# First attention: rotary score products of heads 4 to 7, two heads at a time on the two halves of the rows

## The chip, the cores and the metric

One core of one Trainium2 chip runs the whole program. Times are device microseconds (us) of one execution. In the rows PE is TensorE (matmuls), PEld its weight loads, DVE VectorE, ACT ScalarE, POOL GpSimd, SP the queue that issues most loads.

## What is computed

Two transformer blocks one after the other in fp32, cut here to the part that matters: the attention of the first block's second layer (512 tokens and 256 context tokens, so 768 keys). It has eight heads. Heads 0 to 3 have a head dimension of 128 and share two key/value heads. Heads 4 to 7 have a part without rotary embedding (128 wide, keys of its own for each head) and a rotary part (64 wide, one key for all four heads).

```python
Q_BLOCK = 128; C_HEADS = 4; C_HEAD_DIM = 128; D_HEADS = 4; D_NOPE = 128; D_ROPE = 64; D_V = 128

def block_attention(q, k, v, scale):          # for each block of 128 queries and each head
    sc = einsum('bqhgd,bkhd->bhgqk', qblk, k).astype(float32) * scale
    p = softmax(sc, axis=-1)
    return einsum('bhgqk,bkhe->bqhge', p, v)

def cd_attend(q, qdn, qdr, k, v, kdn, kdr, vd):
    oc = block_attention(q.reshape(b, L, C_KV_HEADS, C_GROUP, C_HEAD_DIM), k, v, C_HEAD_DIM ** -0.5)
    qd = concatenate([qdn, qdr], axis=-1)[:, :, :, None, :]
    kd = concatenate([kdn, broadcast_to(kdr, kdn.shape[:-1] + (D_ROPE,))], axis=-1)
    od = block_attention(qd, kd, vd, (D_NOPE + D_ROPE) ** -0.5)
    return concatenate([oc, od], axis=-1)      # then @ w_out, gate, residual; then the expert layer
```

## The kernel before

The kernel is written engine by engine, with semaphores between the engines and an order written out by hand. `At.todo` lists the 32 steps of the attention: a step `n` is one head `h` and one block `c` of 128 queries. Before the change it goes head by head (0 to 7), four blocks each, so steps 16 to 31 are heads 4 to 7.

On PE the loop in `pe_attention` does, for each `n`: `scores(n)`, then `turn(n - 2)` (six transposes of the probabilities of step n-2), then `values(n - 3)` (six products of 128 columns for step n-3), then `mods(n)`: in one step of four (n = 0, 4, ... 28) a unit of the modulation weights, eight products on four groups of 32 columns, and two steps later the `mod_t` product that turns its row. `scores` writes 768 scores into two PSUM banks (512 and 256 columns). Every fp32 product is carried out as two passes, each with a weight load of its own: the order counts products, the trace passes. For heads 4 to 7 each bank gets two products, the 128-row one and a 64-row rotary one. The rotary queries of heads 4 and 5 lie in one tile (rows 0 to 63 and 64 to 127), those of 6 and 7 in another; the rotary key lies twice, on both halves of the rows of `At.kr`.

The eight PSUM banks go round in turn (`ps.take`): whoever takes a bank waits (`ps.ready`) until the engine that read it eight takes ago has let it go. A step takes two banks for scores, two for transposes, one for values, and every other step one more for `mods`.

The other engines follow step by step. DVE: `scores` (maximum over the two banks), `normal(n - 1)` (reciprocal of the sum of step n-1), `turn(n - 2)` (copies a part of the transposes out of PSUM). ACT: `scores` (the two exponentials, which release the score banks), `turn(n - 2)`, `values(n - 3)` (copies), then the copy of `mods(n)`. POOL: multiplies the probabilities of a step by the reciprocal (L110), for which PE's `turn` waits. When a head is done, `upper` on ACT and `lower` on DVE split its output into two parts for the output product `at_o`, which follows the loop on PE.

Lines of the profile are those of helpers: L92 is every matmul, L95 every transpose, L98 ACT's activations, L102 and L103 copies on ACT and DVE, L106 DVE's two-tensor operations, L110 POOL's product with the reciprocal, L111, L117 and L120 small operations, maxima and reciprocals on DVE.

Of the kernel before, what the change touches and what calls it, by code (L numbers as in the profile page):

```python
# [47 lines left out]
def chunks(T):  # L48
    return [(a, min(512, T - a)) for a in range(0, T, 512)]


class Signal:
# [14 lines left out]
    def of(self, *key):  # L67
        return self.sem, self.value.get(key, 1) if Signal.counting else self.value[key]
# [204 lines left out]
def build(nc, I, out, upto=99):  # L273
# [16 lines left out]
    def signal(name):  # L290
# [21 lines left out]
    ps = Banks([ctx.enter_context(nc.psum_tensor(f"ps{i}", [128, 512], F32))[:, :] for i in range(8)],  # L312
               signal("bank_full"), [signal(f"bank{i}_free") for i in range(8)])
# [61 lines left out]
    def part_upper(e, key):  # L375
        s = wr.at(*key)
        e.wait_ge(*wr.there(*key))
        e.copy(slotR(s, 0, 2048), slot(s, 2048, 2048)).then_inc(*part_hi.up(*key))
# [223 lines left out]
    class F:  # L602
        T = 768
        s = Scratch()
# [1201 lines left out]
    At = Place()  # L1806
# [27 lines left out]

    At.heads = [(3 + m // 2, 128 * (m % 2), 0, 512, At.qT[m], "q_g", True) for m in range(4)]
    At.heads += [(5, 128 * m, a, n, At.kT[m][:, a:a + n], "k_g", a == 0) for m in range(2) for a, n in chunks(768)]
    At.todo = [(h, c) for h in range(8) for c in range(4)]

    sqt = [At.tmp[:, 0:512], At.tmp[:, 512:1024]]
    st_cq = Stat("cq", At.rs[0], sqt, lambda m, a, n: At.cq[m][:, a:a + n], by_tile(3, 512), 512, None)  # L1840
# [25 lines left out]
    def pe_attention(e):  # L1866
# [26 lines left out]
        for kt in range(8):  # L1893
            e.wait_ge(*h_lo.of("at_in", kt))
            for m, o in enumerate(os):
                x = mm3(e, o, parts(("at", 0), 256 * kt + 128 * m), at_in(kt, 0, 512), kt == 0, kt == 7)
# [14 lines left out]
        for n, (j, c, a, w, dst, gain, turns) in enumerate(At.heads):  # L1911
            o = ps.take("head", n, hold=True)
# [11 lines left out]
        for i in range(6):  # L1924
            o = ps.take("v", i)
            e.wait_ge(*ps.ready("v", i))
            e.wait_ge(*lowered("at", 6))
            s = wr.at("at", 6)
            for kt in range(8):
                c = 256 * kt  # L1930
# [8 lines left out]
        for i, m in enumerate((4, 5, 0, 1, 2, 3)):  # L1939
            o = ps.take("uq", m)  # L1940
            e.wait_ge(*ps.ready("uq", m))
            for kt in range(3):
                x = e.matmul(o, weights(("at", "uq"), 768, kt, 128 * m, 128 * m + 128), At.cq[kt], kt == 0, kt == 2)
# [7 lines left out]
        for m in range(4):  # L1951
            for a, n in chunks(768):
                o = ps.take("kn", m, a)
                e.wait_ge(*ps.ready("kn", m, a))
                for kt in range(2):
                    x = e.matmul(o[:, 0:n], weights(("at", "ukv"), 1024, kt, 128 * m, 128 * m + 128), At.ck[kt][:, a:a + n],
                                 kt == 0, kt == 1)
# [10 lines left out]
        e.wait_ge(*dve_step.of("rope", ("qr", 1)))  # L1968

        def scores(n, h, c):  # L1970
            if h < 4:
                terms = [(At.qT[h][:, 128 * c:128 * c + 128], lambda a, w: At.kT[h // 2][:, a:a + w])]
            else:
                g, r0 = h - 4, 64 * (h % 2)
                terms = [(At.qn[g][:, 128 * c:128 * c + 128], lambda a, w: At.kn[g][:, a:a + w]),
                         (At.qr[g // 2][r0:r0 + 64, 128 * c:128 * c + 128], lambda a, w: At.kr[r0:r0 + 64, a:a + w])]
            for a, w in chunks(768):
                o = ps.take("s", n, a)
                e.wait_ge(*ps.ready("s", n, a))
                for i, (l, of) in enumerate(terms):  # L1980
                    x = e.matmul(o[:, 0:w], l, of(a, w), i == 0, i == len(terms) - 1)
                x.then_inc(*ps.fill("s", n, a))

        def turn(n):
            e.wait_ge(*pool_step.of("p_n", n))
# [22 lines left out]
            if u < 12 and n % 4 == 2:  # L2008
                pe_mod_turn(e, At.mod, u)
        for n in range(32 + 3):  # L2010
            if n < 32:
                scores(n, *At.todo[n])
            if 2 <= n < 34:
                turn(n - 2)
            if n >= 3:
                values(n - 3, *At.todo[n - 3])
            mods(n)
# [12 lines left out]
    def act_attention(e):  # L2030
        act_adaln(e, "at_in", 1, 0, 768, st_m[0], at_in)
        for i, d in enumerate((At.rC, At.rS, At.dC, At.dS)):
            e.dma(d, I["rope"][i]).then_inc(*rope_in.up(i, by=16))
        for m in range(3):
            e.wait_ge(*ps.emptied("cq_p", m))
            act_square(e, st_cq, m, 0, 512)
            if m == 1:
                part_upper(e, ("at", 2))
        e.wait_ge(*ps.emptied("ck_p", 0, 0))
        act_norm(e, st_cq)  # L2040
        act_square(e, st_ck, 0, 0, 512)
        e.wait_ge(*ps.emptied("ck_p", 0, 512))
        act_square(e, st_ck, 0, 512, 256)
        part_upper(e, ("at", 3))
        for a, n in chunks(768):
            e.wait_ge(*ps.emptied("ck_p", 1, a))
            act_square(e, st_ck, 1, a, n)
        act_norm(e, st_ck)
        part_upper(e, ("at", 4))

        def norm(n):
            w = At.heads[n][3]
            rs = At.rs[n % 2][:, 0:w]
            e.wait_ge(*ps.emptied("head_s", n))
            e.activation(rs, rs, ACT.Sqrt).then_inc(*rooted.up("head", n))
        for n in range(8):
            if n:
                norm(n - 1)
            w = At.heads[n][3]
            if n >= 2:  # L2060
                e.wait_ge(*ps.filled("head_s", n - 2))
            e.wait_ge(*ps.filled("head", n))
            e.activation(At.sq[n % 2][:, 0:w], ps.ap("head", n)[:, 0:w], ACT.Square).then_inc(*squared.up("head", n))
            if n in (1, 3):
                part_upper(e, ("at", 5 + n // 2))
        for i in range(6):
            e.wait_ge(*ps.filled("v", i))
            e.copy(At.vv[:, 256 * i:256 * i + 256], ps.ap("v", i)[:, 0:256]).then_inc(*ps.empty("v", i))
            if i == 0:
                norm(7)  # L2070
        for m in (4, 5, 0, 1, 2, 3):
            e.wait_ge(*ps.filled("uq", m))
            e.copy((At.qn + At.qr)[m], ps.ap("uq", m)).then_inc(*ps.empty("uq", m))
        for i in range(6):
            e.wait_ge(*ps.filled("vd", i))
            e.copy(At.vd[:, 512 * i:512 * i + 512], ps.ap("vd", i)).then_inc(*ps.empty("vd", i))
        act_mod_begin(e, At.mod)
        e.wait_ge(*dve_step.of("rope", ("qr", 1)))

        def mods(n):  # L2080
            u = 4 + n // 4
            if u < 12 and n % 4 == 0:
                mod_row(e, At.mod, u)
            if u < 12 and n % 4 == 2:
                mod_columns(e, At.mod, u)

        def scores(n, h):
            p, s = At.P[n % 3], At.st[:, 8 * (n % 3):8 * (n % 3) + 8]
            e.wait_ge(*dve_step.of("max", n))
            for i, (a, w) in enumerate(chunks(768)):  # L2090
                e.activation(p[:, a:a + w], ps.ap("s", n, a)[:, 0:w], ACT.Exp, bias=s[:, 2:3],
                             scale=128.0 ** -0.5 if h < 4 else 192.0 ** -0.5, accum_out=s[:, 3 + i:4 + i]).then_inc(
                    *ps.empty("s", n, a))

        def turn(n):
            if n >= 2:
                e.wait_ge(*ps.filled("o", n - 2))
            e.wait_ge(*ps.filled("pt", n, 0))
            e.copy(At.PT[n % 2][:, 0:512], ps.ap("pt", n, 0)).then_inc(*ps.empty("pt", n, 0))

        def values(n, h, c):
            e.wait_ge(*ps.filled("o", n))
            e.copy(At.oT[h][:, 128 * c:128 * c + 128], ps.ap("o", n)[:, 0:128]).then_inc(*ps.empty("o", n))

        def upper(h):
            e.wait_ge(*ps.emptied("o", 4 * h + 3))
            e.copy(At.ohi[h], At.oT[h]).then_inc(*h_hi.up("at_out", h))
        for n in range(32 + 3):
            if n < 32:
                scores(n, At.todo[n][0])  # L2110
            if 2 <= n < 34:
                turn(n - 2)
            if n >= 7 and n % 4 == 3:
                upper((n - 7) // 4)
            if n >= 3:
                values(n - 3, *At.todo[n - 3])
            mods(n)
            if n in (9, 13, 33):
                part_upper(e, ("at_out", {9: 0, 13: 1, 33: 2}[n]))
        upper(7)  # L2120
        for m in range(8):
            e.wait_ge(*ps.emptied("at_o", m))
            act_square(e, st_at, m, 0, 512)
            if m == 2:
                part_upper(e, ("at_out", 3))
        stage_end(e, "at", "dve", "pe")

    def dve_attention(e):
# [97 lines left out]
        def lower(h):  # L2226
            e.wait_ge(*h_hi.of("at_out", h))
            e.tt(At.olo[h], At.oT[h], At.ohi[h].bitcast(F32), SUB).then_inc(*h_lo.up("at_out", h))
        for n in range(32 + 2):
            if n < 32:  # L2230
                scores(n, At.todo[n][0])
            if 1 <= n <= 32:
                normal(n - 1)
            if n >= 2:
                turn(n - 2)
            if n >= 8 and n % 4 == 0:
                lower((n - 8) // 4)
            if n in (10, 14):
                part_lower(e, ("at_out", {10: 0, 14: 1}[n]))
        dve_mod_bias(e, At.mod)  # L2240
        e.wait_ge(*dve_step.of("mod_b", "last"))
        lower(7)
        part_lower(e, ("at_out", 2))
        for m in range(8):
# [1379 lines left out]
```

## Time and profile before

| | |
|---|---|
| median of 3 runs | 3204.3 us (3200.99 to 3208.06) |
| the profiled execution, its own time | 3204.65 us |
| its span in the trace | 3202.9 us |
| PE busy | 2926.3 us (91%) |
| DVE, ACT, POOL busy | 1080.1, 764.3, 509.1 us |
| mean granted clock of TensorE | 0.947 |

The span is 1.75 us shorter than the execution's own time. Busy time of PE includes the tails of pipelined passes, so the start of one group and the start of the next say more than the duration of a group. The granted clock is given in parts of full speed: 1.00 is 2.4 GHz.

### The profile page before, as it was taken

The numbers are of one execution on the slowest core, as the hardware profiler recorded it, in microseconds if no ns is written. First come the engines' busy times: TensorE is split into PE (matmuls) and PEld (weight loads), VectorE is DVE, ScalarE is ACT, GpSimd is POOL, SyncE is SP. The second block draws the span as 40 slices with busy tenths as digits, with TensorE's granted clock in tenths as the row PEclk, the third lists the DMA queues.
The fourth block names the chain that finished last, engine by engine and source line by source line (L and its number), as shares of the span: only waits on it lengthen the run. The fifth ranks groups of instructions, "written<-read, shape, count | busy, mean of one in ns | idle before, by whom it ended". The sixth has DMA issues, their size and how long they took to land.

```text
span 3202.9 us, 36604 instructions
## 1 busy us (share of the span) xinstructions
PE 2926.3 (91%) x15566; PEld 2071.6 (65%) x15566; DVE 1080.1 (34%) x2032; ACT 764.3 (24%) x1365; POOL 509.1 (16%) x505
## 2 busy tenths in 40 slices
PE   6989898899969899979999988999998988999997
PEld 4777755445457665766454447888864766788886
DVE  4973210000044543320000005342388223433334
ACT  4142211011132153311101113222211355322223
POOL 0000132232210043113323311000042132000000
PEclk9989899999979999989999998999999889999998
DMA  6613899999942132369999974332310201223321
GB/s 254 208 43 118 314 386 402 407 388 399 394 150 81 53 119 82 126 230 396 411 414 405 406 297 140 104 104 88 112 48 27 96 1 53 80 92 105 97 79 55
DMA packets 143401, 621.51 MB, mean 194 GB/s; under 512 B 14447, under 2 KB 95471, under 8 KB 109568
## 3 DMA queue, kind: packets, MB, share of 16 engines
q0 software_dynamic: 40160, 403.75, 31.3%
q1 hardware_dynamic: 101920, 210.35, 19.2%
q10 hardware_dynamic: 1152, 4.98, 0.4%
q8 instruction: 127, 2.08, 0.3%
q14 instruction: 42, 0.34, 0.0%
HBM read 612.73 MB, written 29.36 MB: 200 GB/s over the span
## 4 chain that ended last, share of the span: by engine, by line
PE 72%; DMA 16%; DVE 7%; ACT 2%; issue 2%; POOL 1%; SPq 0%; DVEq 0%; POOLq 0%; ACTq 0%
PE ps L92 69%; DMA ring<-in_exp_up,wix 14%; PE ps L95 2%; DVE scr L114 1%; DVE hT L110 1%; DVE scr L106 1%; ACT hT L98 1%; DVE scr L120 1%; DMA ring<-in_mod_w 1%; DMA scr<-in_mod_w 1%; DVE ring_r L106 0%; POOL ring L135 0%; ACT scr L98 0%; DVE hT_r L106 0%; DVE scr L117 0%
## 5 line engine op out<-in xcount | busy, mean ns | idle before, releaser
L92 PE MATMUL ps<-ring,scr 128*64 128x512 f32 (+4 forms) x3392 | 750.0, 546 | 90.0 <-DMA ring<-in_exp_up,wix 65.4
L92 PE MATMUL ps<-ring_r 128*128 128x512 f32 (+1 forms) x2688 | 780.4, 377 | 29.2 <-DVE hT_r L106 21.8
L92 PEld LDWEIGHTS ps<-ring,scr 128*64 128x64 f32 (+2 forms) x3392 | 302.4, 153 | 445.4 <-issue 433.2
L92 PEld LDWEIGHTS ps<-ring_r 128*128 128x128 f32 x2688 | 498.3, 192 | 136.5 <-issue 34.2
L92 PE MATMUL ps<-hT_r,ring_r 128*128 128x512 f32 (+1 forms) x1256 | 474.5, 378 | 0.0
L92 PE MATMUL ps<-scr,ring 128*128 128x128 f32 (+1 forms) x2784 | 333.2, 282 | 21.9 <-DMA ring<-yrows 17.0
L92 PEld LDWEIGHTS ps<-scr,ring 128*128 128x128 f32 x2784 | 321.3, 195 | 31.7 <-issue 30.7
L106 DVE TENSOR_TENSOR scr<-scr,ps 64x512 f32<-64x512 f32 (+1 forms) x76 | 52.5, 690 | 777.6 <-ACT scr L98 466.1
L92 PE MATMUL ps<-scr_r,ring_r 128*128 128x512 f32 x1312 | 306.7, 390 | 0.4 <-issue 0.4
L92 PEld LDWEIGHTS ps<-scr_r,ring_r 128*128 128x128 f32 x1312 | 246.2, 188 | 52.4 <-issue 0.5
L92 PEld LDWEIGHTS ps<-hT_r,ring_r 128*128 128x128 f32 x1256 | 241.2, 192 | 43.4 <-issue 1.9
L106 DVE TENSOR_TENSOR ring_r<-ring,ring_r 128x2048 fp32r<-128x2048 f32 (+1 forms) x98 | 217.0, 2238 | 74.8 <-ACT ring_r L102 74.5
L102 ACT ACTIVATE ring_r<-ring 128x2048 fp32r<-128x2048 f32 (+1 forms) x102 | 186.3, 1834 | 180.7 <-DMA ring<-in_ffn_w 132.4
L102 ACT ACTIVATE scr<-ps 128x512 f32<-128x512 f32 (+3 forms) x216 | 110.2, 525 | 490.1 <-PE ps L92 340.9
L98 ACT ACTIVATE scr<-ps 64x512 f32<-64x512 f32 (+2 forms) x96 | 56.2, 586 | 681.7 <-PE ps L92 681.7
L92 PE MATMUL ps<-ring 128*32 128x512 f32 (+10 forms) x584 | 130.0, 488 | 26.2 <-ACT ring L102 21.3
L103 DVE COPY scr<-ps 128x512 f32<-128x512 f32 (+3 forms) x102 | 54.4, 548 | 260.9 <-PE ps L92 173.7
L95 PEld LDWEIGHTS ps<-KC,scr 64*128 64x128 f32 (+2 forms) x878 | 79.8, 140 | 94.8 <-issue 82.0
L106 DVE TENSOR_TENSOR scr<-hT,ps 128x512 f32<-128x512 f32 x44 | 30.3, 688 | 312.6 <-PE ps L92 312.6
L102 ACT ACTIVATE ring<-ps 128x512 f32<-128x512 f32 (+5 forms) x215 | 85.0, 435 | 192.4 <-PE ps L92 151.1
L92 PEld LDWEIGHTS ps<-ring 64*128 64x128 f32 (+4 forms) x584 | 76.3, 194 | 66.2 <-ACT ring L102 29.6
L95 PE MATMUL ps<-KC,scr 64*128 64x64 f32 (+2 forms) x878 | 107.7, 255 | 5.8 <-DMA scr<-hrows,scr 5.2
(148 smaller groups left out, 2560.6 us busy)
## 6 DMA issues: line engine op xcount, KB each, us to landing
ring<-in_ffn_w SPq DMA_DIRECT2D x66, 1024.0 KB, 5.6
ring<-in_mod_w SPq DMA_DIRECT2D x12, 2048.0 KB, 7.9
ring<-in_mod_w SPq DMA_DIRECT2D x16, 1024.0 KB, 5.0
ring<-in_exp_up SPq DMA_DIRECT2D x4, 2048.0 KB, 12.0
ring<-in_exp_down SPq DMA_DIRECT2D x4, 2048.0 KB, 8.8
scr<-in_mod_w SPq DMA_DIRECT2D x8, 1024.0 KB, 7.8
ring<-in_exp_gate SPq DMA_DIRECT2D x4, 2048.0 KB, 11.4
ring<-in_w_in SPq DMA_DIRECT2D x4, 2048.0 KB, 8.2
```

What stands on the lines that cost most here:

```text
L92: return self.real.matmul(o, l, r, start=start, stop=stop) if self.real else Quiet()
L95: return self.real.transpose(o, i, identity) if self.real else Quiet()
L98: return self.real.activation(o, i, f, **how) if self.real else Quiet()
L102: return self.real.activation(o, i, ACT.Copy) if self.real else Quiet()
L103: return self.real.tensor_copy(o, i) if self.real else Quiet()
L106: return self.real.tensor_tensor(o, a, b, op) if self.real else Quiet()
L110: return self.real.tensor_scalar(o, a, s1, None, op0) if self.real else Quiet()
L114: return self.real.scalar_tensor_tensor(out=o, in0=a, scalar=s, in1=b, op0=op0, op1=op1) if self.real else Quiet()
L120: return self.real.reciprocal(o, i) if self.real else Quiet()
```

## The change

`At.todo` goes through heads 4 and 5 together, block by block (4, 5, 4, 5, ...), then 6 and 7. At every even step from 16 on, PE's new `scores_of_two` computes the scores of two steps at once: for the 512 columns and then for the 256 columns it issues the 128-row products of both heads and then their two 64-row products, the first on rows 0 to 63, the second on rows 64 to 127, into different banks. The four banks are taken at once. The rest of PE's loop keeps its order, as do the loops of DVE, ACT and POOL, except that a head is now done at another step (`At.last`, `At.parts`): heads 4 and 5 after steps 22 and 23, heads 6 and 7 after 30 and 31, so `upper(6)` and `lower(6)` move behind the loop.

```diff
--- before.py
+++ after.py
@@ -1834,7 +1834,10 @@
 
     At.heads = [(3 + m // 2, 128 * (m % 2), 0, 512, At.qT[m], "q_g", True) for m in range(4)]
     At.heads += [(5, 128 * m, a, n, At.kT[m][:, a:a + n], "k_g", a == 0) for m in range(2) for a, n in chunks(768)]
-    At.todo = [(h, c) for h in range(8) for c in range(4)]
+    At.todo = [(h, c) for h in range(4) for c in range(4)]
+    At.todo += [(h + j, c) for h in (4, 6) for c in range(4) for j in range(2)]
+    At.last = {h: max(n for n, x in enumerate(At.todo) if x[0] == h) for h in range(8)}
+    At.parts = {7: 0, 11: 1, 15: 2, 19: 3, 27: 4, 31: 5}
 
     sqt = [At.tmp[:, 0:512], At.tmp[:, 512:1024]]
     st_cq = Stat("cq", At.rs[0], sqt, lambda m, a, n: At.cq[m][:, a:a + n], by_tile(3, 512), 512, None)
@@ -1968,18 +1971,24 @@
         e.wait_ge(*dve_step.of("rope", ("qr", 1)))
 
         def scores(n, h, c):
-            if h < 4:
-                terms = [(At.qT[h][:, 128 * c:128 * c + 128], lambda a, w: At.kT[h // 2][:, a:a + w])]
-            else:
-                g, r0 = h - 4, 64 * (h % 2)
-                terms = [(At.qn[g][:, 128 * c:128 * c + 128], lambda a, w: At.kn[g][:, a:a + w]),
-                         (At.qr[g // 2][r0:r0 + 64, 128 * c:128 * c + 128], lambda a, w: At.kr[r0:r0 + 64, a:a + w])]
             for a, w in chunks(768):
                 o = ps.take("s", n, a)
                 e.wait_ge(*ps.ready("s", n, a))
-                for i, (l, of) in enumerate(terms):
-                    x = e.matmul(o[:, 0:w], l, of(a, w), i == 0, i == len(terms) - 1)
-                x.then_inc(*ps.fill("s", n, a))
+                e.matmul(o[:, 0:w], At.qT[h][:, 128 * c:128 * c + 128], At.kT[h // 2][:, a:a + w], True, True).then_inc(
+                    *ps.fill("s", n, a))
+
+        def scores_of_two(n, h, c):
+            for j in range(2):
+                for a, w in chunks(768):
+                    ps.take("s", n + j, a)
+            for a, w in chunks(768):
+                for j in range(2):
+                    g = h - 4 + j
+                    e.wait_ge(*ps.ready("s", n + j, a))
+                    e.matmul(ps.ap("s", n + j, a)[:, 0:w], At.qn[g][:, 128 * c:128 * c + 128], At.kn[g][:, a:a + w], True, False)
+                for j in range(2):
+                    e.matmul(ps.ap("s", n + j, a)[:, 0:w], At.qr[h // 2 - 2][64 * j:64 * j + 64, 128 * c:128 * c + 128],
+                             At.kr[64 * j:64 * j + 64, a:a + w], False, True).then_inc(*ps.fill("s", n + j, a))
 
         def turn(n):
             e.wait_ge(*pool_step.of("p_n", n))
@@ -2008,8 +2017,10 @@
             if u < 12 and n % 4 == 2:
                 pe_mod_turn(e, At.mod, u)
         for n in range(32 + 3):
-            if n < 32:
+            if n < 16:
                 scores(n, *At.todo[n])
+            elif n < 32 and n % 2 == 0:
+                scores_of_two(n, *At.todo[n])
             if 2 <= n < 34:
                 turn(n - 2)
             if n >= 3:
@@ -2103,20 +2114,21 @@
             e.copy(At.oT[h][:, 128 * c:128 * c + 128], ps.ap("o", n)[:, 0:128]).then_inc(*ps.empty("o", n))
 
         def upper(h):
-            e.wait_ge(*ps.emptied("o", 4 * h + 3))
+            e.wait_ge(*ps.emptied("o", At.last[h]))
             e.copy(At.ohi[h], At.oT[h]).then_inc(*h_hi.up("at_out", h))
         for n in range(32 + 3):
             if n < 32:
                 scores(n, At.todo[n][0])
             if 2 <= n < 34:
                 turn(n - 2)
-            if n >= 7 and n % 4 == 3:
-                upper((n - 7) // 4)
+            if n in At.parts:
+                upper(At.parts[n])
             if n >= 3:
                 values(n - 3, *At.todo[n - 3])
             mods(n)
             if n in (9, 13, 33):
                 part_upper(e, ("at_out", {9: 0, 13: 1, 33: 2}[n]))
+        upper(6)
         upper(7)
         for m in range(8):
             e.wait_ge(*ps.emptied("at_o", m))
@@ -2233,12 +2245,13 @@
                 normal(n - 1)
             if n >= 2:
                 turn(n - 2)
-            if n >= 8 and n % 4 == 0:
-                lower((n - 8) // 4)
+            if n - 1 in At.parts:
+                lower(At.parts[n - 1])
             if n in (10, 14):
                 part_lower(e, ("at_out", {10: 0, 14: 1}[n]))
         dve_mod_bias(e, At.mod)
         e.wait_ge(*dve_step.of("mod_b", "last"))
+        lower(6)
         lower(7)
         part_lower(e, ("at_out", 2))
         for m in range(8):
```

How it moves the instructions, at two places. In these rows `scr,hT` are the score products (a 64-row product is not told apart from a 128-row one), `KC,ring` and `KC,scr` the transposes of `turn`, `ring,hT` 128x128 the products of `values`, `ring` 32x512 the unit of `mods`.

PE, steps 20 and 21, before:

```order
L92 MATMUL ps<-scr,hT 128x512 x2
L92 MATMUL ps<-scr,hT 128x256 [waits bank6_free]
L92 MATMUL ps<-scr,hT 128x256
L95 MATMUL ps<-KC,ring 128x128 [waits bank7_free,pool_step]
L95 MATMUL ps<-KC,ring 128x128 x3
L95 MATMUL ps<-KC,ring 128x128 [waits bank0_free]
L95 MATMUL ps<-KC,ring 128x128
L92 MATMUL ps<-ring,hT 128x128 [waits bank3_free,bank2_free,bank1_free]
L92 MATMUL ps<-ring,hT 128x128 x5
L92 MATMUL ps<-ring 32x512 [waits slot5_landed]
L92 MATMUL ps<-ring 32x512 x7
L92 MATMUL ps<-scr,hT 128x512 x2
```

PE, the same two steps now, the score products of the pair and what follows them:

```order
L92 MATMUL ps<-scr,hT 128x512 [waits bank5_free]
L92 MATMUL ps<-scr,hT 128x512 x3
L92 MATMUL ps<-scr,hT 128x256
L92 MATMUL ps<-scr,hT 128x256 [waits bank0_free]
L92 MATMUL ps<-scr,hT 128x256 x2
L95 MATMUL ps<-KC,ring 128x128 [waits bank1_free,pool_step]
```

The scores of step 21, which stood behind the unit of `mods(20)`, now stand ahead of the transposes of step 18. PE, further on in the same pair, from the values of step 17 to those of step 18:

```order
L92 MATMUL ps<-ring,hT 128x128 [waits bank3_free]
L92 MATMUL ps<-ring,hT 128x128 x5
L92 MATMUL ps<-ring 32x512 [waits bank4_free,slot5_landed]
L92 MATMUL ps<-ring 32x512 x7
L95 MATMUL ps<-KC,scr 128x128 [waits bank5_free,pool_step]
L95 MATMUL ps<-KC,scr 128x128 x3
L95 MATMUL ps<-KC,scr 128x128 [waits bank6_free]
L95 MATMUL ps<-KC,scr 128x128
L92 MATMUL ps<-ring,hT 128x128 [waits bank2_free,bank1_free,bank7_free]
```

No scores stand between the unit and the transposes of step 19 any more, and the values of step 18 (last row) now wait for bank 7, which holds the first scores of step 21 (taken eight takes before) until ACT has read them.

## Rows read from the trace of the kernel before

**Rows 1.** The page: span, and the chain that ended last by engine.

```profile
span 3202.9 us, 36604 instructions
...
PE 72%; DMA 16%; DVE 7%; ACT 2%; issue 2%; POOL 1%; SPq 0%; DVEq 0%; POOLq 0%; ACTq 0%
```

**Rows 2.** Windows: stretch, length, busy PE, PEld, DVE, ACT, POOL, PEclk, DMA share, GB/s.

```profile
1199.00:1295.00 96.00, 96.00 (x510) 55.16 (x509) 34.95 (x100) 34.89 (x107) 34.77 (x17) 1.00 0.21 77
...
1295.00:1302.00 7.00, 5.82 (x51) 5.47 (x50) 1.91 (x6) 3.86 (x10) 3.80 (x2) 1.00 0.01 2
1302.00:1346.00 44.00, 43.94 (x196) 36.10 (x194) 13.36 (x16) 9.60 (x13) 0.00 (x0) 1.00 0.35 120
...
1140.00:1150.00 10.00, 10.00 (x46) 8.11 (x47) 3.21 (x9) 2.77 (x8) 4.26 (x2) 0.66 0.10 34
```

**Rows 3.** Waits of 1199 to 1296 us: who waited for whom, us, times, longest.

```profile
DVE scr L117 <- PE ps L92: 60.4, 32, 3.7
```

**Rows 4.** PE in order of time, end of step 22 to start of step 25.

```profile
1240.73 0.95 PE L92 MATMUL ps<-AM,ring 128*128 128x2 f32 x8
1241.54 3.41 PE L92 MATMUL ps<-scr,hT 128*128 128x512 f32 x8
1244.89 0.87 PE L95 MATMUL ps<-KC,ring 128*128 128x128 f32 x6
1245.60 1.50 PE L92 MATMUL ps<-ring,hT 128*128 128x128 f32 x12
1246.94 3.33 PE L92 MATMUL ps<-scr,hT 128*128 128x512 f32 x8
1250.20 0.87 PE L95 MATMUL ps<-KC,scr 128*128 128x128 f32 x6
...
1252.34 1.92 PE L92 MATMUL ps<-ring 128*32 128x512 f32 x16
1254.20 3.43 PE L92 MATMUL ps<-scr,hT 128*128 128x512 f32 x8
```

**Rows 5.** Weight loads (PEld) of one step's scores, then of one unit.

```profile
1247.89 0.29 PEld L92 LDWEIGHTS ps<-scr,hT 64*128 64x128 f32 x2 [0.76 <-issue]
1248.94 0.30 PEld L92 LDWEIGHTS ps<-scr,hT 128*128 128x128 f32 x2 [0.76 <-issue]
1249.57 0.29 PEld L92 LDWEIGHTS ps<-scr,hT 64*128 64x128 f32 x2 [0.33 <-issue]
...
1252.80 0.13 PEld L92 LDWEIGHTS ps<-ring 128*32 128x32 f32 x4 [0.30 <-issue]
1253.23 0.13 PEld L92 LDWEIGHTS ps<-ring 128*32 128x32 f32 x4 [0.30 <-issue]
```

**Rows 6.** PE in the second attention, from 2662.922 us: in time, then by form.

```profile
2662.92 2.20 PE L92 MATMUL ps<-ring 64*128 64x31 f32 x10
2665.05 0.30 PE L95 MATMUL ps<-KC,scr 128*31 128x128 f32 x1
...
L92 PE MATMUL ps<-ring 64*128 64x512 f32 x8 | 2.2, 612 | 0.0
```

**Rows 7.** ACT and POOL after the scores of step 24, in order of time.

```profile
1251.02 0.69 ACT L98 ACTIVATE ring<-ps,scr 128x512 f32<-128x512 f32 x1 [2.91 <-DVE scr L111]
1251.60 0.19 ACT L98 ACTIVATION_READ_ACCUMULATOR ring<-ps,scr 128x1 f32 x1
...
1251.34 2.20 POOL L110 TENSOR_SCALAR scr<-scr 128x768 f32<-128x768 f32 x1 [3.12 <-DVE scr L120]
...
1254.33 0.60 ACT L102 ACTIVATE ring<-ps 128x512 f32<-128x512 f32 x1 [1.43 <-PE ps L92]
```

**Rows 8.** PE at the end of the loop: transposes of step 30, first output products.

```profile
1296.67 0.88 PE L95 MATMUL ps<-KC,ring 128*128 128x128 f32 x6 [1.18 <-POOL ring L110]
...
1302.16 4.34 PE L92 MATMUL ps<-ring_r 128*128 128x512 f32 x18
```

**Rows 9.** Chain of waits, 1295 to 1352 us: start, us, what.

```profile
1299.73 46.23 PE ps L92 x216
```

## The prediction

> **What bounds the kernel now.** I read the page first, for the whole: the chain that ended last lies for 72% on PE, and the span is 3202.9 us [rows 1]. Next the windows around the change. From 1199 to 1295 us, where steps 16 to 31 run, PE is busy for all 96 us at a granted clock of 1.00, while DVE, ACT and POOL have each some 35 us of work [rows 2]. The list of waits of that stretch tells the same from the other side: DVE waited 60.4 us for PE there [rows 3], and no wait of PE stands in it. So PE's own work sets the pace of the stage, and what follows takes a saving over: the output products hang on PE alone (43.94 of 44.00 us busy, and one piece of 46.23 us in the chain) [rows 2, 9].
>
> **One step.** In order of time a step of heads 4 to 7 is 3.26 us of scores (1246.94 to 1250.20), then transposes, 0.71 us, and values, 1.34 us (1244.89, 1245.60, 1246.94), and in every other step something for the modulation: 0.81 us (1240.73 to 1241.54), or a unit of 1.86 us (1252.34 to 1254.20), with 0.09 us ahead of it [rows 4]. The weight loads show what is inside the 3.26 us: 0.95 us for the 128-row product of 512 columns (from 1246.94), 1.05 us for the rotary one, then 0.63 us for each of the two of 256 columns [rows 4, 5]. A pass of 512 columns takes 0.43 us (1252.80 to 1253.23) [rows 5], one of 256 half of that. Eight passes make 2.58 us. The remaining 0.68 us I put down to the four changes between 128-row and 64-row products, 0.17 us each: at a change the load doesn't run ahead under the last pass, as PEld's idle time ahead of it shows (0.76 and 0.33 us) [rows 5].
>
> **What the change saves on PE.** A pair of heads has 8 passes of 128 rows (2.58 us, as before) and 8 of 64 rows. If two 64-row passes on different halves run side by side, the latter cost 1.29 us and not 2.58 us. The changes of shape are 4 a pair and not 8: 0.68 us and not 1.36 us. A pair then needs 4.55 us where two steps took 6.52 us, so it saves 1.97 us, and eight pairs 15.8 us: 10.3 from working side by side, 5.4 from fewer changes.
>
> Do the halves work side by side in fp32? The second attention already issues 64-row products by turns on the two halves. Four of 512 columns, eight passes, took 2.13 us (2662.92 to 2665.05) [rows 6]; one after the other they would need 8 times 0.43, 3.44 us. The unit is a like case on four groups of columns: 16 passes in 1.86 us [rows 4], four passes' time and a little.
>
> Here a rule speaks against the change. The Trainium skill ("TensorE: Matmul & The Clock Gate", Part 3, The mechanism) says that matmuls start and end strictly in program order and only weight loads are pulled ahead. By that rule the two passes of a product stand together, the first product's second pass would share its time with the second product's first pass and nothing else, and the sum would be -7.6 us instead of the one below. The trace contradicts it: a unit in that order would need nine pass times, 3.9 us, and took 1.86. So I take the full overlap.
>
> **What the change gives back.** The order in which the other engines work stays, but a pair's scores are ready together, and PE comes to the next transposes sooner. I take t = 0 where PE leaves the scores of a pair (m, m+1).
>
> The POOL chain: once a step's scores are done, DVE takes their maximum and then the reciprocal of the step before, and POOL starts on that at 1.14 us (1251.34 against 1250.20) and is done at 3.34 us [rows 4, 7]. PE starts some 0.05 us later. This is step m-1, and PE wants its transposes after those of m-2, the values of m-3 and `mods(m)`: at 2.86 us where that is the small product, at 4.00 us where it is a unit. So PE waits 0.5 us in four of the eight pairs, 2.0 us in all. Before, it came to those transposes after another step's scores, 3.26 us later, and did not wait.
>
> The bank chain, in the other four pairs: the values of m-2 take the bank in which the first scores of m+1 lie. ACT frees it with the exponential of m+1, which on ACT stands behind the copy of the unit's row. The unit ends late: ACT starts that copy at 4.13 us (1254.33) [rows 7]; about 0.5 us later comes the exponential, which lets go of the bank 0.77 us after its start (1251.02 to 1251.79) [rows 7]. That is 5.4 us. PE is there at 4.00 + 0.71 us for the transposes. So PE waits some 0.7 us, four times, 2.8 us. DVE's maximum of m+1 doesn't decide: the exponential of m starts at 0.82 us (1251.02) [rows 7], that of m+1 can't before the row's copy. Behind the waiting values stand only the next pair's scores, which wait for nothing else: their first bank is the other one of m+1, free 0.5 us after the first.
>
> The end of the loop: before, PE waited 1.18 us for POOL ahead of the transposes of step 30 [rows 8]. Now POOL has both last steps back to back, and PE reaches them after 2.05 us of other work each; POOL needs 2.20, which leaves two waits of about 0.1 us. A gain of 1.0 us. `upper(6)` and `lower(6)` now come behind the loop. The output products start with head 0 and need head 6 after 18 passes, 4.2 us later (1302.16 and 4.34 us) [rows 8]; a copy of 0.6 us more on ACT and 0.7 us on DVE is hidden by that, and costs up to 1.3 us if it isn't. Loads: the unit's weights wait for the same slot as before and DMA is at a share of 0.21 [rows 2]; nothing.
>
> **Sum:** -15.8 + 2.0 + 2.8 - 1.0 = -12.0 us. The profiled execution took 3204.65 us, so 3192.65; it lies 0.35 us above the median of 3204.3 us, so the forecast is **3192.3 us**. Bounds of the unknown waits: none, -16.8 us; each twice as long, -7.2 us.
>
> **Rivals.**
>
> 1. *Passes in strict order.* Only one pass of four is shared: a pair saves 0.43 + 0.215 us less, 5.2 us in all; as the second head ends a pass after the first, the POOL waits shrink by 0.2 us each. -12.0 + 5.2 - 0.8 = -7.6 us, 3196.7 us. For it: a product's two passes are issued together. Against it: rows 4 and 6, as above. Chance 0.14.
>
> 2. *No overlap at all*, the change doing nothing but saving changes of shape: -12.0 + 10.3, and the POOL waits nearly vanish (-1.7): -3.4 us, 3200.9 us. If each change of half cost 0.17 us as a change of shape does, six a pair, 8.2 us more: +4.8 us. For it: the products here accumulate onto others in the same bank, which those of rows 6 don't. Against it: the rest of rows 6. Chance 0.12.
>
> 3. *The new waits cost the clock.* From 1140 to 1150 us the clock was granted at 0.66 on average [rows 2], a mixture of its two levels, 2.4 and 1.2 GHz; such a stretch loses 3.4 us of PE's work. If the eight new waits brought as many, +27.2 - 12.0 = +15.2 us, 3219.5 us; from four such stretches on the kernel is slower. Against it: the wait of 1.18 us at 1295.5 us is longer than any new one, PE was busy for only 5.82 of 7.00 us there, and the clock stayed at 1.00 through the next 44 us [rows 2, 8]. Chance 0.04.
>
> 4. *Longer waits than I count*, because DVE or ACT is behind by one more operation than I followed: around -6.5 us, 3197.8 us. Chance 0.08.
>
> **How the numbers follow.** The forecast case has the remaining 0.62. A measurement of this kernel can tell about 0.2%, 6.4 us, from no change. Faster by more than that: the 0.62, most of rival 1 (0.12) and half of rival 4 (0.04), 0.78. Slower by more: 0.04. Within: 0.18. The range goes from 3187.5 us (no waits at all) to 3199.5 us, which takes in rivals 1 and 4 and leaves out 2 and 3.
>
> **What the profile after would show.** Between the weight loads of a pair's first and last shape change the 512-column rotary products of both heads take 1.05 us together, those of 256 columns 0.63, and the pair's scores start 4.55 us before its transposes; by rival 1 it would be 5.2 us, by rival 2 5.8 us or more. PE waits some 0.5 us for POOL (L110) in every other pair, and some 0.7 us for ACT (L98) in the pairs with a unit; the wait of 1.18 us is gone; four steps take 21.3 us instead of 24.0 (four times 5.31, 0.81 and 1.95). The granted clock stays at 1.00 up to the output products, and all later stages keep their length. I am wrong if rotary loads of the two halves are a pass apart, if a wait of PE is over 1 us, or if the stage is shorter and the whole is not.

## The result, and the profile after

Twenty executions of the changed kernel have a median of 3190.09 us, twenty of the kernel before 3204.95 us. The ratio is 0.9959 with a 95% interval of 0.9946 to 0.9973, so 13 us faster (9 to 17). The forecast was 3192.3 us. The profiled execution took 3189.21 us.

The page of the changed kernel, the lines that answer to [rows 1]:

```profile
span 3187.4 us, 36609 instructions
...
PE 71%; DMA 16%; DVE 7%; ACT 2%; issue 2%; POOL 1%; SPq 0%; DVEq 0%; POOLq 0%; ACTq 0%
```

The bound is still PE. What moved is seen in its order of time; here is PE of the changed kernel from the start of step 16, then the end of a pair with a unit and a pair without one, then the end of the loop (start, duration, group, idle time before it and who ended it):

```profile
1198.47 4.64 PE L92 MATMUL ps<-scr,hT 128*128 128x512 f32 x16
...
1228.51 0.88 PE L95 MATMUL ps<-KC,scr 128*128 128x128 f32 x6
1229.97 1.60 PE L92 MATMUL ps<-ring,hT 128*128 128x128 f32 x12 [0.58 <-ACT ring L98]
1231.41 4.64 PE L92 MATMUL ps<-scr,hT 128*128 128x512 f32 x16
1235.97 0.87 PE L95 MATMUL ps<-KC,scr 128*128 128x128 f32 x6
1236.68 1.50 PE L92 MATMUL ps<-ring,hT 128*128 128x128 f32 x12
1238.02 0.95 PE L92 MATMUL ps<-AM,ring 128*128 128x2 f32 x8
1239.37 0.88 PE L95 MATMUL ps<-KC,ring 128*128 128x128 f32 x6 [0.39 <-POOL ring L110]
...
1284.49 0.87 PE L95 MATMUL ps<-KC,ring 128*128 128x128 f32 x6
1285.20 1.50 PE L92 MATMUL ps<-ring,hT 128*128 128x128 f32 x12
1286.67 0.87 PE L95 MATMUL ps<-KC,scr 128*128 128x128 f32 x6
1287.38 2.84 PE L92 MATMUL ps<-ring,hT 128*128 128x128 f32 x24
1289.98 4.37 PE L92 MATMUL ps<-ring_r 128*128 128x512 f32 x18
```

The scores of a pair take 4.56 us (1231.41 to 1235.97). Before, the two steps of such a pair took 6.61 us: 3.35 us for the one behind the small product (1241.54 to 1244.89) and 3.26 us for the one behind values (1246.94 to 1250.20) [rows 4]. Two waits are new, one of 0.58 us for ACT in each pair with a unit and one of 0.39 us for POOL in each of the others; the wait of 1.18 us at the end of the loop [rows 8] is gone.

What PE waits for, in the same two pairs. ACT copies the unit's row first and then takes the exponential that frees the bank for PE's values at 1229.97:

```profile
1228.65 0.60 ACT L102 ACTIVATE ring<-ps 128x512 f32<-128x512 f32 x1 [1.44 <-PE ps L92]
1229.14 0.68 ACT L98 ACTIVATE ring<-ps,scr 128x512 f32<-128x512 f32 x1
```

DVE takes the reciprocal behind the next pair's maximum, and POOL, which starts on it, is done at 1239.32, just ahead of PE's transposes at 1239.37:

```profile
1236.07 0.42 DVE L117 TENSOR_REDUCE scr<-ps 128x1 f32<-128x256 f32 x1 [1.00 <-PE ps L92]
...
1236.85 0.16 DVE L120 RECIPROCAL scr<-scr 128x1 f32<-128x1 f32 x1
...
1237.11 2.21 POOL L110 TENSOR_SCALAR ring<-ring,scr 128x768 f32<-128x768 f32 x1 [6.27 <-DVE scr L120]
```

From here on **the stage** is the time from the first score product of step 16 to the first output product: 1198.55 to 1302.16 us before, 103.6 us, and 1198.47 to 1289.98 us now, 91.5 us. It is 12.1 us shorter.

The weight loads of the same kind of pair, to be laid beside [rows 5]:

```profile
1243.23 0.30 PEld L92 LDWEIGHTS ps<-scr,hT 64*128 64x128 f32 x4 [0.76 <-issue]
1244.29 0.73 PEld L92 LDWEIGHTS ps<-scr,hT 128*128 128x128 f32 x4 [0.76 <-issue]
1245.35 0.30 PEld L92 LDWEIGHTS ps<-scr,hT 64*128 64x128 f32 x4 [0.33 <-issue]
1245.98 0.64 PEld L95 LDWEIGHTS ps<-KC,scr 128*128 128x128 f32 x6 [0.33 <-issue]
```

Four 64-row loads stand where two stood, and the rotary products of both heads are done in 1.06 and 0.63 us, just as long as those of one head before. In the group of forms the same number of passes keeps PE busy for half the time (from 1199 us to the end of the loop; the kernel before, then the changed one):

```profile
L92 PE MATMUL ps<-scr,hT 64*128 64x512 f32 x32 | 18.0, 641 | 0.0
```

```profile
L92 PE MATMUL ps<-scr,hT 64*128 64x512 f32 x32 | 9.0, 641 | 0.0
```

And in the windows the granted clock stayed at 1.00 in spite of the waits:

```profile
1199.00:1283.00 84.00, 80.12 (x500) 51.16 (x499) 32.66 (x98) 34.32 (x106) 34.82 (x17) 1.00 0.25 88
```

### The profile page after: what moved, and what is told of

Same layout as the page of the kernel before. It is cut to its first block, busy times and chain, and to the rows that moved or that the text cites. A ratio compares the mean times of both kernels' runs of the same rounds, so it can differ in the third digit from the quotient of the medians.

```text
span 3187.4 us, 36609 instructions
## 1 busy us (share of the span) xinstructions
PE 2909.5 (91%) x15566; PEld 2064.2 (65%) x15566; DVE 1079.2 (34%) x2032; ACT 764.7 (24%) x1365; POOL 510.3 (16%) x505
## 4 chain that ended last, share of the span: by engine, by line
PE 71%; DMA 16%; DVE 7%; ACT 2%; issue 2%; POOL 1%; SPq 0%; DVEq 0%; POOLq 0%; ACTq 0%
PE ps L92 69%; DMA ring<-in_exp_up,wix 14%; PE ps L95 2%; DVE scr L114 1%; DVE hT L110 1%; ACT hT L98 1%; DVE scr L106 1%; DVE scr L120 1%; DMA ring<-in_mod_w 1%; DMA scr<-in_mod_w 1%; ACT scr L98 0%; POOL ring L135 0%; DVE ring_r L106 0%; DVE hT_r L106 0%; DVE scr L117 0%
## 5 line engine op out<-in xcount | busy, mean ns | idle before, releaser
L95 PE MATMUL ps<-KC,scr 64*128 64x64 f32 (+2 forms) x878 | 107.4, 254 | 7.3 <-DMA scr<-hrows,scr 5.5
```

The costliest lines, as they stand in the source:

```text
L95: return self.real.transpose(o, i, identity) if self.real else Quiet()
```

## The experiments

The stage is read from each trace in the same way; it came out the same to 0.1 us whenever a kernel was run again (91.5 us for the changed kernel both times, 103.6 us for the one before both times), while whole executions differ by several us. So the small effects are judged by the stage, and the whole by intervals where there are enough executions. Each ratio is to executions of the kernel before that were made beside that version (medians of 3203.93 us for `e1_same_half` and `e2_head_by_head`, 3201.35 us for `e8_act_dve` and `e7_all`), so it is not the quotient of two medians of this table. All of them at a glance, in us:

| | stage | median, or one execution | ratio to before, 95% |
|---|---|---|---|
| before | 103.6 | 3204.95 | |
| changed | 91.5 | 3190.09 | 0.9959 (0.9946 to 0.9973) |
| `e1_same_half` | 101.1 | 3208.55 | 1.0008 (0.9993 to 1.0023) |
| `e2_head_by_head` | 107.4 | 3210.21 | 1.0019 (1.0006 to 1.0032) |
| `e9_steps_only` | 103.6 | 3198.28 (one) | |
| `e3_two_changes` | 89.0 | 3194.49 (one) | |
| `e4_act_order` | 88.1 | 3188.33 (one) | |
| `e5_dve_order` | 90.9 | 3182.72 (one) | |
| `e8_act_dve` | 86.0 | 3185.01 | 0.9950 (0.9934 to 0.9966) |
| `e7_all` | 83.4 | 3184.77 | 0.9948 (0.9930 to 0.9967) |
| `e6_by_half` | 89.0 | 3188.18 (one) | |

### What the change is made of

`e1_same_half` takes the side-by-side work away and leaves everything else. (The second head's scores are computed with the first head's rotary queries.)

```diff
-e.matmul(ps.ap("s", n + j, a)[:, 0:w], At.qr[h // 2 - 2][64 * j:64 * j + 64, 128 * c:128 * c + 128],
-         At.kr[64 * j:64 * j + 64, a:a + w], False, True)
+e.matmul(ps.ap("s", n + j, a)[:, 0:w], At.qr[h // 2 - 2][0:64, 128 * c:128 * c + 128],
+         At.kr[0:64, a:a + w], False, True)
```

> The changed kernel, but the second head's rotary product also takes rows 0 to 63 (so its scores use the first head's rotary queries; the rest is as it is): same order, same four changes of shape a pair, nothing to run side by side. The stage is counted from the first score product of step 16 to the first output product: 103.6 us before, 91.5 us after the change. Theory (side by side is worth 1.3 us a pair, fewer changes of shape 0.7 us): a pair's scores take 5.9 us instead of 4.57, the wait for POOL vanishes, the wait for the bank in the pairs with a unit stays at 0.6 us, the stage is 101.5 us, so 2 us below the kernel before and 10 us above the changed one. Rival (what counts is the order, or the changes of shape alone): stage at or near 91.5 us, scores of a pair under 5 us.

PE in this version, in order of time:

```profile
1232.26 5.91 PE L92 MATMUL ps<-scr,hT 128*128 128x512 f32 x16
1238.10 0.87 PE L95 MATMUL ps<-KC,scr 128*128 128x128 f32 x6
1238.81 1.50 PE L92 MATMUL ps<-ring,hT 128*128 128x128 f32 x12
1240.15 0.95 PE L92 MATMUL ps<-AM,ring 128*128 128x2 f32 x8
1241.06 0.87 PE L95 MATMUL ps<-KC,ring 128*128 128x128 f32 x6
```

Scores of 5.84 us a pair, no wait for POOL in the list, a stage of 101.1 us: 9.6 us of the 12.1 come from the two halves working side by side. (Shorter delays are left in these pairs: 0.91 us from the small product to the transposes where it takes 0.81, and 0.98 us from the transposes to the values at 1242.04 where it takes 0.71.) What is left is a stage 2.5 us shorter than before, which the whole kernel did not confirm (its interval goes from -2 to +7 us), so that remainder rests on the trace of the stage alone.

`e2_head_by_head` issues the pair's scores at the same place, but each head for itself:

```diff
-for a, w in chunks(768):
-    for j in range(2):
+for j in range(2):
+    for a, w in chunks(768):
         ...
         e.matmul(..., At.qn[g]..., At.kn[g]..., True, False)
-    for j in range(2):
         e.matmul(..., At.qr[...]..., At.kr[...]..., False, True)
```

> The changed kernel with the pair's scores issued at once, but one head after the other, each as before the change (128-row, 64-row, 128-row, 64-row): eight changes of shape a pair and no 64-row products next to each other. Theory: scores of a pair 6.6 us, the stage some 107.5 us, 4 us longer than before the change, because the new place of the scores brings waits (0.6 us for the bank in each pair with a unit, up to 0.4 us in the others) that nothing pays for. The kernel as a whole 3 to 5 us slower than before. Rival (the new place of the scores costs nothing by itself, the waits are only those of a faster PE): stage at 103.6 us.

The stage took 107.4 us, and the whole kernel was slower than before (ratio 1.0019, both ends of the interval above 1). Two rows of its PE show the two waits for ACT's exponential that the new place of the scores brings:

```profile
1234.52 1.60 PE L92 MATMUL ps<-ring,hT 128*128 128x128 f32 x12 [0.58 <-ACT ring L98]
...
1246.52 1.60 PE L92 MATMUL ps<-ring,hT 128*128 128x128 f32 x12 [0.22 <-ACT scr L98]
```

So computing two steps' scores ahead is not free: with the same products it costs 3.8 us. The change pays that out of the 16.4 us that its scores save (eight times 6.61 - 4.56). Against `e1_same_half`, which has four changes of shape a pair fewer, a pair's scores are 0.78 us longer (6.62 and 5.84), 0.195 us for each of the four; the stage is 6.3 us longer.

`e9_steps_only` keeps the new order of steps and the old way to compute scores (step by step, one head at a time).

> Only the order of the steps is changed (heads 4 and 5 by turns, then 6 and 7; head 6 finished behind the loop), each step's scores where they were before, one head at a time. Theory: the stage keeps its 103.6 us within 0.5, the later splitting of head 6 is hidden by the first output products, which start at once and run without a gap. Rival (the later end of head 6 shows): up to 1.3 us more, as a wait of PE for DVE in the first output product.

A stage of 103.6 us, and its only wait of PE is the old one of 1.18 us. Head 6 is needed only after 18 passes of the output products, and these took 4.21 us (4.18 before); PE does not wait in the output products either. So the order of heads and the later end of head 6 cost nothing.

### Changes of shape

`e3_two_changes` issues the 64-row products of both banks at the end of the pair:

```diff
 for a, w in chunks(768):
     for j in range(2):
         ... 128-row products ...
+for a, w in chunks(768):
     for j in range(2):
         ... 64-row products ...
```

> The changed kernel with all four 128-row products of a pair first (512, 512, 256, 256 columns) and then the four 64-row ones: two changes of shape a pair instead of four. Theory: scores of a pair 4.57 - 2 x 0.19 = 4.2 us, eight pairs 3.0 us; the first head's 512 columns are complete later, so DVE's maxima and with them POOL end 0.2 us later against PE, the wait for POOL grows from 0.39 to 0.6 us four times; stage 89.3 us against 91.5. Rival (a change of shape costs nothing, the 0.17 us are something else): scores of a pair stay at 4.57 us, stage 91.5 us or, with the longer wait, 92.4 us.

```profile
1234.09 0.88 PE L95 MATMUL ps<-KC,scr 128*128 128x128 f32 x6
1234.80 1.50 PE L92 MATMUL ps<-ring,hT 128*128 128x128 f32 x12
1236.14 0.95 PE L92 MATMUL ps<-AM,ring 128*128 128x2 f32 x8
1237.65 0.88 PE L95 MATMUL ps<-KC,ring 128*128 128x128 f32 x6 [0.55 <-POOL ring L110]
...
1239.70 4.24 PE L92 MATMUL ps<-scr,hT 128*128 128x512 f32 x16
1243.87 0.87 PE L95 MATMUL ps<-KC,scr 128*128 128x128 f32 x6
```

Scores of 4.17 us instead of 4.56, two changes of 0.195 us each, and a wait for POOL of 0.55 us instead of 0.39, since the first head's last maximum comes later against PE. The stage is 89.0 us.

`e6_by_half` has the same products in another order: both of the first half, then both of the second.

> The version with two changes of shape a pair, but its four 64-row products go by halves: first head (rows 0 to 63) 512 and 256 columns, then second head (rows 64 to 127) 512 and 256. How far ahead can the array take work for the free half? If only the passes next in line start (a later one waits until all before it have started), the second half starts with the last pass of the first: 64-row products 1.29 - 0.22 + 1.29 = 2.4 us a pair instead of 1.3, scores of a pair 5.3 us, stage some 97 us against 89.0 us when they alternate. If the array takes passes for a free half out of order, as far as four passes ahead: 1.3 us, stage 89 us.

The stage is 89.0 us again, and the scores of a pair took 4.17 us (1235.74 to 1239.91). Its weight loads:

```profile
1238.41 0.31 PEld L92 LDWEIGHTS ps<-scr,hT 64*128 64x128 f32 x4 [0.33 <-issue]
1238.95 0.20 PEld L92 LDWEIGHTS ps<-scr,hT 64*128 64x128 f32 x2 [0.23 <-issue]
1239.38 0.20 PEld L92 LDWEIGHTS ps<-scr,hT 64*128 64x128 f32 x2 [0.23 <-issue]
1239.91 0.64 PEld L95 LDWEIGHTS ps<-KC,scr 128*128 128x128 f32 x6 [0.33 <-issue]
```

All eight 64-row passes, 1.29 us of them on each half, are done in 1.50 us, change of shape included. One half after the other would take 2.4 us or more. The loads stand four, two and two together, as they should if each half has its own at each point. The first pass of the second half, fifth in the program, did not wait for the four ahead of it.

### The two waits

`e4_act_order` moves one group of instructions on ACT: in a pair the second exponential stands ahead of `mods`.

```diff
-            if n < 32:
+            if n < 16 or n < 32 and n % 2 == 0:
                 scores(n, At.todo[n][0])
             ...
+            if 16 <= n < 32 and n % 2 == 0:
+                scores(n + 1, At.todo[n + 1][0])
             mods(n)
```

> The changed kernel, but on ACT the exponential of a pair's second step stands ahead of the copy of the modulation row and no longer behind it. Theory (in the pairs with a unit PE waits for that exponential through a bank, and it is late only because ACT waits for the unit): the four waits of 0.58 us for ACT (L98) are gone, with the weight load they left uncovered 0.1 us more each; stage 88.6 us against 91.5 us, the waits for POOL of 0.39 us stay. Rival (ACT itself is the limit there, or DVE's maximum): a wait of 0.3 us or more stays ahead of the same values, stage 90.5 us or more.

`e5_dve_order` moves the reciprocal of a pair's second step on DVE ahead of the next pair's maxima.

```diff
+            early_normal = 18 <= n < 32 and n % 2 == 0
+            if early_normal:
+                normal(n - 1)
             if n < 32:
                 scores(n, At.todo[n][0])
-            if 1 <= n <= 32:
+            if 1 <= n <= 32 and not early_normal:
                 normal(n - 1)
```

> The changed kernel, but on DVE the reciprocal of a pair's second step stands ahead of the next pair's maxima and no longer behind them, so POOL can start 5 us sooner. Theory: the four waits of 0.39 us for POOL (L110) are gone, but PE then comes to the next values sooner and waits there for ACT's exponential through the bank, 0.4 us: the stage is 91.1 us, next to the 91.5 us of the changed kernel; one wait hides the other. Rival (the waits are independent): stage 91.5 - 4 x 0.39 = 89.9 us and no new wait.

`e8_act_dve` has both.

> Both changes of order together, ACT's exponential ahead of the row copy and DVE's reciprocal ahead of the next maxima; the scores as in the changed kernel. Theory: no wait of PE over 0.2 us is left in the pairs; stage 86.7 us, 1.9 us below the one with ACT's order alone, where DVE's order alone brought 0.4 us. Rival (waits independent, as they add up): 91.5 - 2.9 - 1.6 = 87.0 us with DVE's order alone at 89.9 us; the two are told apart by the run with DVE's order alone, and here by whether a third wait (a bank held by ACT's second half) shows up, which would leave the stage above 87.5 us.

With ACT's order alone the stage is 88.1 us, 3.4 us less, and the only waits left in the list are those for POOL:

```profile
1238.56 0.88 PE L95 MATMUL ps<-KC,ring 128*128 128x128 f32 x6 [0.39 <-POOL ring L110]
```

With DVE's order alone it is 90.9 us, only 0.6 us less. The waits for POOL are gone, but two groups on, where PE did not wait in the changed kernel, it now waits for ACT's exponential:

```profile
1233.11 0.85 PE L95 MATMUL ps<-KC,ring 128*128 128x128 f32 x6
1234.18 1.60 PE L92 MATMUL ps<-ring,hT 128*128 128x128 f32 x12 [0.22 <-ACT scr L98]
```

With both, the stage is 86.0 us, 5.5 us less and not 3.4 + 0.6, and no wait of PE is listed in the pairs. The wait for POOL had covered a second one.

`e7_all` adds the two changes of shape of `e3_two_changes` to both orders.

> Both changes of order and only two changes of shape a pair. Theory: stage 84.2 us, 19.4 us below the kernel before and 7.3 us below the changed one; waits of PE in the pairs under 0.15 us each; the whole kernel some 19 us faster than before (ratio about 0.994), since the later stages keep their length. Rival (the gain ends where ACT or POOL take over): waits of 0.3 us or more for L98 or L110 in each pair and a stage above 86 us.

The stage is 83.4 us and PE is busy without a break (75.00 of 75.00 us, clock 1.00):

```profile
1197.00:1272.00 75.00, 75.00 (x495) 51.64 (x494) 31.29 (x98) 32.88 (x102) 33.91 (x17) 1.00 0.28 99
```

The whole kernel is 17 us faster than before (10.6 to 22.4). The stage puts it 8 us ahead of the changed kernel; the intervals of the two against the kernel before overlap, so that part is shown for the stage, not for the whole.

### The rest of the program

The profiled execution of the changed kernel was 15.4 us shorter than that of the kernel before, and the stage gave 12.1. Most of the rest, 3.0 us, lies in the second attention, which the change doesn't touch.

> The changed kernel once more, as it is. The stage of the change is 91.5 us again within 0.2. The second attention, whose code no version here changes, took 164.7 us in the trace before and 161.7 us after the change. If that difference comes from the change, it is 161.7 us again and 164.7 us for the kernel before; if it comes from when the clock is granted, which differs from execution to execution, both take any value between some 159 and 170 us, as the traces of the other versions do.

> The kernel before once more, as it is: stage 103.6 us within 0.2; second attention 164.7 us if its length belongs to the version, anywhere from 159 to 170 us if it belongs to the execution.

From its first 64-row product to its last 31-row one the second attention took 161.7 us in the first trace of the changed kernel and 167.7 in the second, 164.7 and 164.1 us in the two of the kernel before, and in the other versions anything from 158.8 to 169.6 us. It belongs to the execution: the same program, the changed kernel, took both 161.7 and 167.7 us. Here are the windows over just this stretch, `e2_head_by_head`, the changed kernel's two traces, and `e7_all`, with the granted clock third from the end:

```profile
2537.24:2696.04 158.80, 133.10 (x783) 99.86 (x784) 54.53 (x301) 92.57 (x286) 53.87 (x96) 0.90 0.02 6
```

```profile
2522.86:2684.56 161.70, 135.89 (x783) 102.52 (x784) 55.06 (x301) 92.66 (x286) 53.80 (x96) 0.88 0.02 6
```

```profile
2512.48:2680.18 167.70, 143.15 (x784) 109.25 (x784) 55.14 (x301) 93.00 (x286) 53.55 (x96) 0.83 0.02 6
```

```profile
2515.43:2685.03 169.60, 146.68 (x783) 110.74 (x784) 55.05 (x301) 93.11 (x286) 53.81 (x96) 0.81 0.02 6
```

The work of DVE, ACT and POOL is the same to 1 us, and the stretch is the longer the lower the clock that PE was granted over it, from 0.90 to 0.81 of full speed, that is 2.4 GHz for a longer or a shorter part of it. A part alone doesn't tell: the first 20 us were at 0.84 in the trace of 167.7 us and at 0.69 in that of 161.7. Why the grant differs is open. In `e3_two_changes` the second attention took 169.5 us, 7.8 us more than in the profiled execution of the changed kernel; that is why this one execution took 3194.49 us, 5.3 us longer, with a stage that is 2.5 us shorter.

## Why the prediction was right

**The bound.** PE set the pace of the stage, and the saving passed through: the stage lost 12.1 us, and the time between its end and the second attention stayed (1233.2 us before, 1232.9 us after).

**The saving on PE, -15.8 us: it was 16.4.** Foreseen were 4.55 us for a pair's scores, and 4.56 were measured. What was too small is what they are set against. The prediction took 3.26 us for every step before the change, 6.52 for two; but a step behind the small product or a unit took 3.35 to 3.37 us, which [rows 4] show at 1241.54 and 1254.20. So a pair saves 2.05 us and not 1.97. The split was foreseen as 10.3 us for working side by side and 5.4 for changes of shape. `e1_same_half` gives 1.28 us a pair for the first, 10.2 us (5.84 against 4.56), of which 9.6 us show in the stage, since that version is held up a little less by the others. `e3_two_changes` gives 0.195 us for a change, 32 changes 6.2 us, and the two make the 16.4. The prediction's 0.17 is a mean over the four changes of a step, and the last of them, into the transposes, costs less ahead of them: three at 0.195 leave 0.10 of the 0.68 us for it. `e2_head_by_head`, where seven of eight changes lie inside, agrees: 5.16 us of passes, 7 times 0.195 and 0.10 make the 6.62 us of its scores.

**The POOL chain, 0.5 us four times.** From the end of the small product to the transposes it was 0.54 us: 1238.02 and 0.81 us make 1238.83, and they began at 1239.37, 2.1 us in all; the row itself names 0.39 us of waiting. `e5_dve_order` took away its cause, and it went.

**The bank chain, 0.7 us four times: it was 0.85.** Between the transposes at 1228.51 and the values at 1229.97 lie 1.46 us, of which 0.71 are the transposes, so 0.75 us; the row names 0.58 us. The prediction left out that the values themselves then take 1.44 us (1229.97 to 1231.41) and not 1.34. That makes 0.85 us a pair and 3.4 us in all, which is just what `e4_act_order` gains. That run took away the cause, the exponential behind the row's copy, and the wait went.

**The end of the loop, -1.0 us: it was -1.2.** The wait of 1.18 us is gone. The two expected waits of 0.1 us are there, though too short to be listed: from the values at 1285.20 to the transposes at 1286.67 it is 1.47 us and not 1.34. But one of about 0.1 us stood there before the change too, so from the values of step 28 to the first output product it takes 6.96 us now and took 8.17.

**The rivals.** Strict order of the passes would have given 5.2 us for a pair's scores, no overlap 5.8. The first falls with 4.56 us, and more clearly with `e6_by_half` (1.50 us where strict order needs 2.4). The Trainium skill's rule of a strict program order ("TensorE: Matmul & The Clock Gate", Part 3, The mechanism) does not hold here, since a pass of the free half started ahead of earlier ones. A dearer change of half did not appear either. The clock did not fall after the new waits (1.00 in the stage). Longer waits than counted came only in the bank chain, 0.15 us in each pair with a unit.

**The size.** 12.0 us were foreseen, the stage shows 12.1, the ratio says 13 (9 to 17). The terms were less exact than their sum: measured, they are -16.4 + 2.1 + 3.4 - 1.2 = -12.1 us, so 0.8 us more gained and 0.7 us more given back than foreseen. That the two nearly cancel is luck; the mechanism was the one described. That the medians stand 14.9 us apart is within what whole executions scatter.

## What to carry to other kernels

Two fp32 products that need only half of the rows cost here the price of one if they stand next to each other on different halves, and each change between full and half shape costs something of its own; so collect the half-height products of several heads in one place. Bringing work forward to do so shifts who is late: follow the semaphores and the buffers of the neighbours (here the copy ahead of an exponential on ACT, the maxima ahead of a reciprocal on DVE), because a small reordering on an engine with time to spare can give back what the fast engine loses, here 5.5 us of 91.5. Remove such waits together: one alone gave 0.6 us, since it hid another.

## What the runs showed of the hardware

- An fp32 product of 512 columns is two passes of 0.43 us, and two of them on rows 0 to 63 and 64 to 127 take the time of one: 1.06 us for both heads' rotary products with one change of shape, 1.05 us for one head's.
- A change between 128-row and 64-row products costs 0.195 us of PE (4.56 against 4.17 us for a pair, two changes fewer). The load ahead of it did not run under the last pass in the rows shown (PEld idle for 0.76 or 0.33 us before each such load, before the change and after).
- Passes of different halves did not keep the order of the program: in `e6_by_half` four passes of one half stand ahead of the four of the other, and all eight were done in 1.50 us, so both halves started together.
- The clock granted to the same instructions differs from execution to execution: over the second attention 0.90 to 0.81 on average, and this part took 158.8 to 169.6 us, the longer the lower the clock.
